# Differential attention's last heads: parts of dense units and output products placed around each transposition and ahead of each value product

## The chip, the core and the metric

The kernel runs on one core of a Trainium2 chip. The metric is the device time of one execution in microseconds. The kernel before takes 2173.66 us (median of three runs, 2173.38 to 2174.19). The core's engines have queues of their own and meet only at semaphores: TensorE (PE in the profile) multiplies and transposes into the eight PSUM banks, VectorE (DVE), ScalarE (ACT) and GpSimd (POOL) do the rest, and SyncE's queue (SP) starts the weight transfers.

## The reference, cut to what matters

The reference is a chain of a sparse-attention and latent-attention block, a recurrent (HGRN2) layer, two squared-ReLU MLPs and one layer of differential attention, for 512 positions of width 1024 in float32. The change is in the differential attention, which has 8 heads; the last two lines are in full what follows it before the last MLP.

```python
q = (h @ w_q).reshape(B, S, DIFF_HEADS, 2, DIFF_HEAD_DIM)
logits = einsum('bqhmd,bshmd->bhmqs', q, k) * scale + bias
logits = where(allowed, logits, NEG_INF)
p = softmax(logits, axis=-1)
attn = p[:, :, 0] - lam * p[:, :, 1]
o = einsum('bhqs,bshe->bqhe', attn, v)
o = rms_norm(o, subln_w) * (1.0 - lam_init)
mix = o.reshape(B, S, D_MODEL) @ w_out
h = h + rms_norm(mix, b_norm_post[bi])
```

## The kernel before, in words

Every engine's program is written out by hand, in the order in which its function calls stand; there is no planner. A float32 product of weights and activations is split: each weight unit (128x1024) is copied by ScalarE into a high part (`split` on ScalarE, line 935) and subtracted by VectorE into a low part (`split` on VectorE, line 1546), and TensorE multiplies three times (high by high, high by low, low by high). The split units lie in a ring of three buffers, `WHL`. The raw weights come by DMA into two slots of two units each, `raw`; a slot is free again when the low part of its second unit is made.

Differential attention goes head by head. For head h TensorE does, in this order:

- `map_scores(h, i)`, i = 0, 1, 2 (line 3004): the two maps' scores in pieces, read from PSUM by `biased_maps` on VectorE (line 2145), then `map_exp` on ScalarE (line 1397) and `joined` on VectorE (lines 2153 to 2161), which makes one map out of two.
- `turn_map(h, i)`, i = 0, 1, 2 (line 3017): ten 128x128 transpositions of the joined map, in groups of 4, 4 and 2. All three groups write the same bank, `TURN` (bank 1), so each waits until the one before has been copied out: the first two groups by ScalarE (`map_evac`, line 935, 128x512), the third by VectorE (`turned_map`, line 2170, 128x256).
- `map_values(h)` (line 3034): ten products of the turned map with the values, after all three copies.
- `map_out_turn(h)` (line 3042): four transpositions of the head's normed output. It needs the sums of squares (`map_squares`, ScalarE, line 1439), the root (`map_stats`, GpSimd, lines 721 to 725) and the scaling (`gated_map`, VectorE, line 2178). ScalarE then copies it out (`map_out_evac`), makes its high part (`map_x_high`), and VectorE its low part (`map_x_low`, line 2199). That is the left operand of the output product.

Between these small steps TensorE does dense work. For heads 0 to 5 this is `kv_dense(d)`, d = 0 to 39: the projections to keys, queries (`kq`, lines 2286 to 2288) and values (`dv`, lines 2984 to 2986), each call 12 products 128x512. The table `D_AT` says which calls belong to which head; `dense_at(h, i)` gives the i-th of up to six. Heads 0, 1, 2 have six, heads 3 and 4 five (d = 26 to 30 and 31 to 35), head 5 four (36 to 39): three go with the score pieces, the rest after the transpositions. So a head with five has nothing between its third transposition and its value product, and head 5 has nothing after its second transposition either. When a call with odd d is done, ScalarE (`kv_out`) copies a key or query out and splits a unit, and VectorE (`kv_low`) makes a low part.

For heads 6 and 7 the dense work is the output product `out_product(k, tts)` (lines 2882 to 2884), 12 products for all four row tiles, k = 0 to 15. For k below 8 it is the k-th head's output times the left half of `w_out`, and it waits for `map_x_low(k)`; k = 8 and up are the same heads with the right half. Two neighbouring k share a weight unit.

Of the kernel before, what the change touches and what calls it, by code (L numbers as in the profile page):

```python
# [37 lines left out]
KD = D // P  # L38
# [226 lines left out]
def program(nc, t, out):  # L265
    with ExitStack() as ctx:
# [146 lines left out]
        def dense_at(h, i):  # L413

            d = D_AT[h][0] + i if h < len(D_AT) else 0
            return d if h < len(D_AT) and d < D_AT[h][1] else None


        ss, rstd = small[:, 0:4], small[:, 4:8]
# [508 lines left out]
        def _(act):  # L928
# [5 lines left out]
            def copy(dst, src, **k):  # L934
                return a.activation(dst, src, ACT.Copy, **k)  # L935
# [464 lines left out]
            def map_evac(h, i):  # L1400

                if h >= 2 and i == 0:
                    act.wait_ge(pv_done, J_DIFF + h - 1)
                act.wait_ge(pt_psum, 3 * (J_DIFF + h) + i + 1)
                copy(map_turned(h)[:, 512 * i:512 * (i + 1)], TURN[:, :]).then_inc(pt_act, 1)
# [12 lines left out]
            def kv_out(d):  # L1418

                if d is not None and d % 2:  # L1420
                    name, u = DENSE_KV[d // 8], d // 2 % 4
                    if name[:2] == "kq":
                        key_query(name, u)
                    split(unit_at["dv0", 0] + d // 2 + HL)
# [31 lines left out]
            for h in range(HH - 2):  # L1456
                for i in range(3):
                    map_exp(h + 1, i)
                    if i == 2 and h:
                        map_out_evac(h - 1)  # L1460
                    kv_out(dense_at(h, i))
                map_evac(h, 0)
                kv_out(dense_at(h, 3))
                map_evac(h, 1)
                kv_out(dense_at(h, 4))
                kv_out(dense_at(h, 5))
                if h == HH - 3:
                    for k in range(4):
                        map_x_high(k)
                map_squares(h)  # L1470
# [27 lines left out]
        def _(vec):  # L1498
# [219 lines left out]
            for i, quarter in enumerate((0.25, 0.0)):  # L1718
                k = cs[:, 3 + i, :, :]
# [36 lines left out]
            for i in range(8):  # L1756
                s, tt = divmod(i, TT)
# [186 lines left out]
            for i in range(16):  # L1944
                half, rest = divmod(i, 8)
# [220 lines left out]
            def turned_map(h):  # L2166
                if h >= 2:
                    vec.wait_ge(pv_done, J_DIFF + h - 1)
                vec.wait_ge(pt_psum, 3 * (J_DIFF + h) + 3)
                v.tensor_copy(map_turned(h)[:, 1024:1280], TURN[:, 0:256]).then_inc(pt_vec, 1)  # L2170
# [21 lines left out]
            def kv_low(d):  # L2192

                if d is not None and d % 2:
                    split(w0 + d // 2 + 2)
# [17 lines left out]
            for h in range(HH - 2):  # L2213
                bias_ready(h + 1)
                for i in range(3):
                    biased_maps(h + 1, i)
                    if i == 0 and h == 4:
                        values_evac(1, (2, 3))
                    if i == 1 and h:
                        gated_map(h - 1)  # L2220
                    kv_low(dense_at(h, i))
                for i in (3, 4, 5):
                    kv_low(dense_at(h, i))
                turned_map(h)
                joined(h + 1)
                if h == 3:
                    values_evac(1, (0, 1))
# [30 lines left out]
        def _(pe):  # L2258
# [610 lines left out]
            def out_product(k, tts=range(TT), name="h_out"):  # L2869

                half, j, u = k // KD, k % 2, k // 2
                wh, wl = (y.rearrange("p (k c) -> p k c", k=2)[:, j, :] for y in unit(name, u))
                k %= KD
                if half == 0:
                    pe.wait_ge(x_lo, x0[name] + k + 1)
                for tt in tts:
                    if half == k == 0:
                        _, reader, at = GT["hg1" if name == "h_out" else "kq3"]
                        pe.wait_ge(ps_free[reader], at + tt + 1)
                    xh, xl = (y[:, k, tt * P:(tt + 1) * P] for y in (HXh, HXl))  # L2880
                    b = ybank(tt, half)
                    m.matmul(b[:, :], xh, wh, start=(k == 0), stop=False)  # L2882
                    m.matmul(b[:, :], xh, wl, start=False, stop=False)  # L2883
                    ins = m.matmul(b[:, :], xl, wh, start=False, stop=(k == KD - 1))  # L2884
                if tts[-1] == TT - 1 and j:
                    ins.then_inc(*((ring_used, 1) if u < KD - 1 else (y_full, 1)))
                elif half and k == KD - 1:
                    ins.then_inc(y_full, 1)
# [58 lines left out]

            norm_halves(5)

            def kv_dense(d):  # L2950

                c, half = divmod(d, 2)
                block, u = divmod(c, 4)
                name = DENSE_KV[block]

                def bank_free(i):

                    if half or u and name[:2] == "dv":
                        return
                    if block:  # L2960
                        _, reader, at = GT[DENSE_KV[block - 1]]
                        pe.wait_ge(ps_free[reader], at + i + 1)
                    elif i >= 2:
                        pe.wait_ge(ps_free["act"], GT["kq0"][2] + 2 * i - 3)

                if name[:2] == "kq":
                    w = [y.rearrange("p (k c) -> p k c", k=KD) for y in unit(name, u)]
                    bank_free(u)
                    for k in range(4 * half, 4 * half + 4):
                        ins = feature_product(DB[u], w, (HXh, HXl), k)  # L2970
                    if half:
                        ins.then_inc(ps_full, 1)
                    return
                wh, wl = (y.rearrange("p (k c) -> p k c", k=2) for y in unit(name, u))
                for tt in (2 * half, 2 * half + 1):
                    if u == 0:
                        if block:
                            _, reader, at = GT[DENSE_KV[block - 1]]
                            pe.wait_ge(ps_free[reader], at + tt + 1)
                        elif tt >= 2:  # L2980
                            pe.wait_ge(ps_free["act"], GT["kq0"][2] + 2 * tt - 3)
                    for k in range(2):
                        xh, xl = (y[:, 2 * u + k, tt * P:(tt + 1) * P] for y in (HXh, HXl))
                        m.matmul(DB[tt][:, :], xh, wh[:, k, :], start=(u + k == 0), stop=False)
                        m.matmul(DB[tt][:, :], xh, wl[:, k, :], start=False, stop=False)
                        ins = m.matmul(DB[tt][:, :], xl, wh[:, k, :], start=False, stop=(u == 3 and k == 1))
                    if u == 3:
                        ins.then_inc(ps_full, 1)
                    elif tt == TT - 1:
                        ins.then_inc(ring_used, 1)  # L2990
# [47 lines left out]
            def map_out_turn(h):  # L3038

                pe.wait_ge(on_ready, HH + h + 1)  # L3040
                for tt in range(TT):
                    ins = m.transpose(OUT[:, tt * P:(tt + 1) * P], on_d[:, h % 2, tt, :], ident[:, :])
                ins.then_inc(ot_psum, 1)

            def dense_step(h, i):

                d = dense_at(h, i)
                if d is not None:
                    kv_dense(d)
# [8 lines left out]
            for h in range(HH - 2):  # L3058
                for i in range(3):
                    map_scores(h + 1, i)  # L3060
                    if i == 2 and h:
                        map_out_turn(h - 1)
                    dense_step(h, i)
                for i in range(3):
                    turn_map(h, i)
                    dense_step(h, 3 + i)
                map_values(h)
            map_scores(7, 0)
            out_product(0, name="d_out")
# [2 lines left out]
            map_scores(7, 2)  # L3072
            map_out_turn(5)
            turn_map(6, 0)
            out_product(2, name="d_out")
            turn_map(6, 1)
            turn_map(6, 2)
            map_values(6)
            turn_map(7, 0)
            out_product(3, name="d_out")  # L3080
            turn_map(7, 1)
            map_out_turn(6)
            out_product(4, name="d_out")
            turn_map(7, 2)
            map_values(7)
            out_product(5, name="d_out")
            out_product(6, name="d_out")
            for k in (KD, KD + 1):
                out_product(k, (0, 1), "d_out")
            map_out_turn(7)  # L3090
            for k in (KD, KD + 1):
                out_product(k, (2,), "d_out")
            out_product(7, name="d_out")
# [37 lines left out]
```

## Time and profile before

| | |
|---|---|
| median of three runs | 2173.66 us |
| the profiled execution's own time | 2171.69 us |
| its span, first to last instruction | 2169.9 us |
| mean granted TensorE clock | 0.995 |
| TensorE busy, share of the span | 97% |
| VectorE, ScalarE, GpSimd busy | 49%, 38%, 13% |
| DMA, mean rate over the span | 88 GB/s |

A row of the timeline has the start in us from the span's start, the time in us that the instructions take together, engine, line, operation, output and input names, count, and in brackets the engine's idle time before it with what ended it. TensorE's rows overlap: a product of 512 columns is shown with 390 ns and the next starts earlier, so steps are measured from start to start. "Issue" as a releaser says that nothing the profile shows was seen to end the wait.

### The profile page before, as it was taken

What the parts mean: (1) busy time and instruction counts of PE and PEld (TensorE: products, weight loads), DVE (VectorE), ACT (ScalarE), POOL (GpSimd) and SP (SyncE); (2) the same over time, 40 slices, a digit from 0 to 9 for tenths busy, and PEclk for the clock granted to TensorE, in tenths of its full rate; (3) what the DMA queues carried; (4) which work ended last, traced back from release to release, by engine and by line L of the source; (5) the groups of instructions that cost most, each with busy time, mean ns of one, the idle gap of its engine ahead of it and who ended that gap; (6) DMA issues with size and microseconds to landing.
All of it is one profiled execution on the core that took longest, in us unless ns stands there. A gap on an engine that the chain in (4) does not pass through costs nothing.

```text
span 2169.9 us, 27018 instructions
## 1 busy us (share of the span) xinstructions
PE 2096.1 (97%) x10814; PEld 1722.8 (79%) x10814; DVE 1057.5 (49%) x1762; ACT 829.0 (38%) x1521; POOL 280.0 (13%) x337
## 2 busy tenths in 40 slices
PE   7999989999999999899999999999999989999998
PEld 6987557888887877788887888888877768888887
DVE  4442846565555343666665533433555546333334
ACT  3144745353333233423233422322445545223222
POOL 8300000010000000223232100000433101000000
PEclk9999999999999999999999999999999999999999
DMA  6435512323332222221212223222332212332222
GB/s 145 93 113 90 66 40 59 117 72 95 97 97 96 97 96 79 88 78 59 77 60 78 75 96 97 98 97 96 112 107 88 75 52 88 97 97 97 98 97 78
DMA packets 172346, 192.00 MB, mean 88 GB/s; under 512 B 22866, under 2 KB 141949, under 8 KB 172221
## 3 DMA queue, kind: packets, MB, share of 16 engines
q1 hardware_dynamic: 168301, 176.30, 26.1%
q0 software_dynamic: 3904, 13.97, 3.5%
q8 instruction: 86, 1.41, 0.3%
q14 instruction: 39, 0.32, 0.0%
q10 hardware_dynamic: 16, 0.00, 0.0%
HBM read 182.91 MB, written 7.34 MB: 88 GB/s over the span
## 4 chain that ended last, share of the span: by engine, by line
PE 91%; DVE 3%; ACT 2%; DMA 1%; issue 1%; POOL 1%; SPq 0%; POOLq 0%; ACTq 0%; DVEq 0%
PE bank L2416 25%; PE bank L2286 12%; PE bank L2288 12%; PE bank L2287 12%; PE bank L2826 2%; PE bank L2353 2%; PE bank L2354 2%; PE bank L2355 2%; PE bank L2861 1%; PE bank L2863 1%; PE bank L2862 1%; PE bank L2882 1%; PE bank L2884 1%; PE bank L2883 1%; PE bank L2555 1%
## 5 line engine op out<-in xcount | busy, mean ns | idle before, releaser
L1546 DVE TENSOR_TENSOR WHL<-raw,WHL 128x1024 fp32r<-128x1024 f32 x310 | 393.6, 1271 | 501.7 <-ACT WHL L935 501.4
L935 ACT ACTIVATE WHL<-raw 128x1024 fp32r<-128x1024 f32 x310 | 326.4, 1054 | 542.8 <-PE bank L2416 344.4
L2286 PE MATMUL bank<-HXh,WHL 128*128 128x512 f32 x1152 | 454.6, 395 | 2.7 <-DVE BIG L1762 1.6
L2288 PE MATMUL bank<-HXh,WHL 128*128 128x512 f32 x1152 | 449.7, 390 | 0.0
L2287 PE MATMUL bank<-HXl,WHL 128*128 128x512 f32 x960 | 373.6, 389 | 0.0
L2416 PE MATMUL bank<-WHL,HXh 128*128 128x512 f32 x1376 | 369.3, 390 | 0.7 <-ACT BIG L935 0.7
L2416 PEld LDWEIGHTS bank<-WHL,HXh 128*128 128x128 f32 x1376 | 257.7, 188 | 55.9 <-issue 1.9
L2286 PEld LDWEIGHTS bank<-HXh,WHL 128*128 128x128 f32 x1152 | 217.0, 188 | 51.0 <-issue 6.9
L2288 PEld LDWEIGHTS bank<-HXh,WHL 128*128 128x128 f32 x1152 | 216.8, 188 | 46.2
L2416 PE MATMUL bank<-WHL,HXl 128*128 128x512 f32 x688 | 211.9, 389 | 0.0
L2287 PEld LDWEIGHTS bank<-HXl,WHL 128*128 128x128 f32 x960 | 180.3, 188 | 36.6
L2416 PEld LDWEIGHTS bank<-WHL,HXl 128*128 128x128 f32 x688 | 129.1, 188 | 27.0
L2120 DVE TENSOR_TENSOR BIG<-PB 128x512 f32<-128x512 f32 x64 | 44.3, 692 | 192.1 <-ACT PB L1095 192.1
L737 POOL TENSOR_SCALAR small<-small 128x1 f32<-128x1 f32 x24 | 9.4, 393 | 954.0 <-ACT PB L1031 954.0
L1095 ACT ACTIVATE PB<-bank 128x512 f32<-128x512 f32 x64 | 38.2, 597 | 230.8 <-PE bank L2288 214.1
L1976 DVE SCALAR_TENSOR_TENSOR PB<-bank,cols,PB 128x511 f32<-128x511 f32 x88 | 65.9, 749 | 101.6 <-ACT PB L1310 100.0
L704 POOL TENSOR_TENSOR raw<-raw,cols 128x1024 f32<-128x1024 f32 x24 | 46.9, 1969 | 385.5 <-DMA raw<-in_b_w_q_dram 376.6
L1310 ACT ACTIVATE PB<-bank,cols 128x512 f32<-128x512 f32 x44 | 34.3, 781 | 142.0 <-PE bank L2288 136.1
L2416 PE MATMUL bank<-WHL,HX2h 128*128 128x512 f32 x352 | 83.2, 390 | 1.9 <-DVE HX2h L1555 1.7
L2416 PEld LDWEIGHTS bank<-WHL,HX2h 128*128 128x128 f32 x352 | 65.9, 188 | 16.4 <-issue 2.1
L2287 PE MATMUL bank<-HX2l,WHL 128*128 128x512 f32 x192 | 75.7, 394 | 0.0
L882 POOL TENSOR_TENSOR PB<-BIG,PB 128x512 f32<-128x512 f32 x24 | 40.1, 1671 | 174.7 <-PE bank L2826 121.7
(318 smaller groups left out, 3245.1 us busy)
## 6 DMA issues: line engine op xcount, KB each, us to landing
raw<-in_mlp_w_up_dram SPq DMA_DIRECT2D x64, 512.0 KB, 4.6
raw<-in_mlp_w_down_dram SPq DMA_DIRECT2D x64, 512.0 KB, 4.4
raw<-in_w_up_dram SPq DMA_DIRECT2D x44, 512.0 KB, 5.1
raw<-in_a_w_in_dram SPq DMA_DIRECT2D x32, 512.0 KB, 4.6
raw<-in_w_in_dram SPq DMA_DIRECT2D x24, 512.0 KB, 4.8
raw<-in_w_down_dram SPq DMA_DIRECT2D x22, 512.0 KB, 4.1
raw<-in_w_kv_dram SPq DMA_DIRECT2D x16, 512.0 KB, 4.2
rel_dram<-GB POOLq DMA_DIRECT2D x1, 5120.0 KB, 53.8
```

Source lines behind the costliest of these rows:

```text
L704: g.tensor_tensor(w, w, cols[:, c:c + nk].unsqueeze(2).to_broadcast([P, nk, D // nk]), ALU.mult).then_inc(w_scaled, 1)
L935: return a.activation(dst, src, ACT.Copy, **k)
L1546: v.tensor_tensor(dst(1), src, dst(0).bitcast(F32), ALU.subtract).then_inc(w_lo, 1)
L1976: ins = v.scalar_tensor_tensor(out=y[:, sh:T], in0=b[:, 0:T - sh], scalar=tapcol(tap, f), in1=y[:, sh:T], op0=ALU.mult, op1=ALU.add)
L2120: v.tensor_tensor(uT[:, f, :], r, r, ALU.mult).then_inc(u_ready, 1)
L2286: m.matmul(b[:, :], w[0][:, k, :], x[0][:, k, :], start=(k == 0), stop=False)
L2287: m.matmul(b[:, :], w[0][:, k, :], x[1][:, k, :], start=False, stop=False)
L2288: return m.matmul(b[:, :], w[1][:, k, :], x[0][:, k, :], start=False, stop=(k == KD - 1))
L2353: m.matmul(b[:, sl], wh[:, k, :], HXh[:, k, sl], start=(k == 0), stop=False)
L2354: m.matmul(b[:, sl], wh[:, k, :], HXl[:, k, sl], start=False, stop=False)
L2355: ins = m.matmul(b[:, sl], wl[:, k, :], HXh[:, k, sl], start=False, stop=(k == KD - 1))
L2416: ins = m.matmul(ybank(tt, h)[:, :], x, w[:, h * HALF:(h + 1) * HALF], start=(k == 0 and i == 0), stop=(k == nk - 1 and i == 2))
```

## The change

Nothing is computed differently and no instruction's shape changes. Two things move.

First, in the heads with fewer than six dense units the last unit is taken in two parts of six products each, one behind the transposition before its old place and one behind the transposition after. `parted(h)` names the position: 4 for heads 3 and 4 (d = 30 and d = 35), 3 for head 5 (d = 39), none for the others. ScalarE does head 5's `kv_out(39)` behind its second copy, and VectorE does `turned_map(h)` ahead of the `kv_low` of the parted position (that changes an instruction's place for heads 4 and 5; d = 30 has no `kv_low` work).

Second, in heads 6 and 7 the output products are halved by row tiles, (0, 1) and (2, 3), and spread; `out_product(4)` moves ahead of `map_out_turn(6)`, and a half of k = 9 moves behind `map_out_turn(7)`.

```diff
+        def parted(h):
+            return 5 - sum(dense_at(h, i) is None for i in (4, 5)) if dense_at(h, 5) is None else None
...
                 map_evac(h, 0)
-                kv_out(dense_at(h, 3))
+                if parted(h) != 3:
+                    kv_out(dense_at(h, 3))
                 map_evac(h, 1)
+                if parted(h) == 3:
+                    kv_out(dense_at(h, 3))
...
                 for i in (3, 4, 5):
+                    if i == (parted(h) or 6):
+                        turned_map(h)
                     kv_low(dense_at(h, i))
-                turned_map(h)
+                if parted(h) is None:
+                    turned_map(h)
                 joined(h + 1)
...
-            def kv_dense(d):
+            def kv_dense(d, part=None):
...
-                    bank_free(u)
-                    for k in range(4 * half, 4 * half + 4):
+                    if not part:
+                        bank_free(u)
+                    for k in range(4 * half + (2 if part == 1 else 0), 4 * half + (2 if part == 0 else 4)):
                         ins = feature_product(DB[u], w, (HXh, HXl), k)
-                    if half:
+                    if half and part != 0:
                         ins.then_inc(ps_full, 1)
...
-                for tt in (2 * half, 2 * half + 1):
+                for tt in (2 * half, 2 * half + 1) if part is None else (2 * half + part,):
...
                 for i in range(3):
                     turn_map(h, i)
-                    dense_step(h, 3 + i)
+                    if i + 2 == parted(h):
+                        kv_dense(dense_at(h, i + 2), 1)
+                    if i + 3 == parted(h):
+                        kv_dense(dense_at(h, i + 3), 0)
+                    else:
+                        dense_step(h, 3 + i)
                 map_values(h)
...
             turn_map(6, 0)
-            out_product(2, name="d_out")
+            out_product(2, (0, 1), "d_out")
             turn_map(6, 1)
+            out_product(2, (2, 3), "d_out")
             turn_map(6, 2)
+            out_product(3, (0, 1), "d_out")
             map_values(6)
             turn_map(7, 0)
-            out_product(3, name="d_out")
+            out_product(3, (2, 3), "d_out")
             turn_map(7, 1)
+            out_product(4, name="d_out")
             map_out_turn(6)
-            out_product(4, name="d_out")
             turn_map(7, 2)
+            out_product(5, (0, 1), "d_out")
             map_values(7)
-            out_product(5, name="d_out")
+            out_product(5, (2, 3), "d_out")
             out_product(6, name="d_out")
-            for k in (KD, KD + 1):
-                out_product(k, (0, 1), "d_out")
+            out_product(KD, (0, 1), "d_out")
             map_out_turn(7)
+            out_product(KD + 1, (0, 1), "d_out")
```

TensorE, head 5, before: the end of unit 39 (bank 2), the second and third group of transpositions (bank 1, together x6), the value product (bank 3), the scores of head 7 (banks 5 and 7) and the first output product (bank 4).

```order
L2286 MATMUL bank2<-HXh,WHL 128x512
L2287 MATMUL bank2<-HXl,WHL 128x512
L2288 MATMUL bank2<-HXh,WHL 128x512
L3017 MATMUL bank1<-ident,GM 128x128 x6
L3034 MATMUL bank3<-BIG,PB 128x128 x10
L3004 MATMUL bank5<-BIG 128x512
L3004 MATMUL bank7<-BIG 128x512
L2882 MATMUL bank4<-WHL,HXh 128x512
```

The same place in the changed kernel, from the second group of transpositions on (its line numbers are some ten higher).

```order
L3028 MATMUL bank1<-ident,GM 128x128 x4
L2296 MATMUL bank2<-HXh,WHL 128x512
L2297 MATMUL bank2<-HXl,WHL 128x512
L2298 MATMUL bank2<-HXh,WHL 128x512
L2296 MATMUL bank2<-HXh,WHL 128x512
L2297 MATMUL bank2<-HXl,WHL 128x512
L2298 MATMUL bank2<-HXh,WHL 128x512
L3028 MATMUL bank1<-ident,GM 128x128 x2
L3045 MATMUL bank3<-BIG,PB 128x128 x10
```

Six of unit 39's twelve products now stand between the second and the third group; between the third group and the value product there is still nothing.

VectorE, head 5, before: the low part of a weight unit, the copy of the third group (line 2170), the joining of head 6's maps (2153 to 2161) and the low parts of the first two heads' outputs (2199).

```order
L1546 TENSOR_TENSOR WHL<-raw,WHL 128x1024
L2170 COPY PB<-bank1 128x256
L2153 RECIPROCAL small<-small 128x8
L2156 SCALAR_TENSOR_TENSOR small<-small 128x4
L2161 SCALAR_TENSOR_TENSOR GM<-PB,small,GM 128x512
L2161 SCALAR_TENSOR_TENSOR GM<-PB,small,GM 128x384
L2161 SCALAR_TENSOR_TENSOR GM<-PB,small,GM 128x128
L2161 SCALAR_TENSOR_TENSOR GM<-PB,small,GM 128x256
L2199 TENSOR_TENSOR HXl<-BIG,HXh 128x512 x2
```

VectorE, head 5, in the changed kernel, from the copy on.

```order
L2177 COPY PB<-bank1 128x256
L1553 TENSOR_TENSOR WHL<-raw,WHL 128x1024
L2160 RECIPROCAL small<-small 128x8
L2163 SCALAR_TENSOR_TENSOR small<-small 128x4
L2168 SCALAR_TENSOR_TENSOR GM<-PB,small,GM 128x512
L2168 SCALAR_TENSOR_TENSOR GM<-PB,small,GM 128x384
L2168 SCALAR_TENSOR_TENSOR GM<-PB,small,GM 128x128
L2168 SCALAR_TENSOR_TENSOR GM<-PB,small,GM 128x256
L2206 TENSOR_TENSOR HXl<-BIG,HXh 128x512 x2
```

The low part of the weight unit has moved from ahead of the copy to behind it, and so ahead of the joining and of the two low parts of the output.

TensorE, head 7, in the changed kernel: the last products of `out_product(4)` (bank 2), the transposition of head 6's output (bank 3) head 7's third group and the first product of k = 5. Before, the bank-3 row stood directly behind the row of four on bank 1, and the twelve products behind it.

```order
L2892 MATMUL bank2<-WHL,HXh 128x512
L2893 MATMUL bank2<-WHL,HXh 128x512
L2894 MATMUL bank2<-WHL,HXl 128x512
L3053 MATMUL bank3<-ident,PB 128x128 x4
L3028 MATMUL bank1<-ident,GM 128x128 x2
L2892 MATMUL bank4<-WHL,HXh 128x512
```

## Rows read from the trace of the kernel before

**Rows 1.** The page: busy time by engine, and the chain that ended last by engine.

```profile
PE 2096.1 (97%) x10814; PEld 1722.8 (79%) x10814; DVE 1057.5 (49%) x1762; ACT 829.0 (38%) x1521; POOL 280.0 (13%) x337
...
PE 91%; DVE 3%; ACT 2%; DMA 1%; issue 1%; POOL 1%; SPq 0%; POOLq 0%; ACTq 0%; DVEq 0%
```

**Rows 2.** Timeline of PE, heads 2 and 3.

```profile
1672.96 0.38 PE L3017 MATMUL bank<-ident,GM 128*128 128x128 f32 x2
1675.93 2.39 PE L3034 MATMUL bank<-BIG,PB 128*128 128x128 f32 x20
1678.25 1.13 PE L3004 MATMUL bank<-BIG 64*128 64x512 f32 x4
...
1693.40 0.60 PE L3017 MATMUL bank<-ident,GM 128*128 128x128 f32 x4
...
1695.00 0.39 PE L2986 MATMUL bank<-WHL,HXl 128*128 128x512 f32 x1
...
1695.91 0.39 PE L2984 MATMUL bank<-WHL,HXh 128*128 128x512 f32 x1
...
1696.59 0.38 PE L3017 MATMUL bank<-ident,GM 128*128 128x128 f32 x2
1697.60 2.47 PE L3034 MATMUL bank<-BIG,PB 128*128 128x128 f32 x20 [0.63 <-issue]
```

**Rows 3.** Timeline of PE, head 5 to the first output product.

```profile
1734.13 0.60 PE L3017 MATMUL bank<-ident,GM 128*128 128x128 f32 x4
...
1737.34 0.60 PE L3017 MATMUL bank<-ident,GM 128*128 128x128 f32 x4
1739.62 0.44 PE L3017 MATMUL bank<-ident,GM 128*128 128x128 f32 x2 [1.68 <-ACT PB L935]
1740.69 3.72 PE L3034 MATMUL bank<-BIG,PB 128*128 128x128 f32 x20 [0.63 <-issue]
...
1745.75 0.50 PE L2882 MATMUL bank<-WHL,HXh 128*128 128x512 f32 x1
```

**Rows 4.** Timeline of PE, heads 6 and 7.

```profile
1753.85 0.60 PE L3017 MATMUL bank<-ident,GM 128*128 128x128 f32 x4
...
1759.41 2.47 PE L3034 MATMUL bank<-BIG,PB 128*128 128x128 f32 x20 [0.63 <-issue]
...
1767.76 0.66 PE L3042 MATMUL bank<-ident,PB 128*128 128x128 f32 x4 [2.19 <-DVE PB L2178]
...
1773.61 2.47 PE L3034 MATMUL bank<-BIG,PB 128*128 128x128 f32 x20 [0.63 <-issue]
...
1786.88 0.47 PE L2882 MATMUL bank<-WHL,HXh 128*128 128x512 f32 x1 [0.78 <-DVE HXl L2199]
```

**Rows 5.** Two windows: busy time by engine, then granted clock, DMA share, GB/s.

```profile
1740.00:1745.00 5.00, 4.37 (x23) 3.96 (x24) 4.04 (x11) 2.16 (x7) 0.00 (x0) 0.67 0.01 3
1770.00:1775.00 5.00, 4.37 (x21) 3.47 (x21) 1.02 (x2) 0.00 (x0) 0.00 (x0) 0.76 0.01 3
```

**Rows 6.** Timeline of ACT: copies of transposed maps of heads 5, 6 and 7.

```profile
1738.98 0.59 ACT L935 ACTIVATE PB<-bank 128x512 f32<-128x512 f32 x1
...
1755.40 0.58 ACT L935 ACTIVATE PB<-bank 128x512 f32<-128x512 f32 x1
...
1763.74 0.59 ACT L935 ACTIVATE PB<-bank 128x512 f32<-128x512 f32 x1
```

**Rows 7.** Timeline of DVE, head 5.

```profile
1731.91 1.23 DVE L1546 TENSOR_TENSOR WHL<-raw,WHL 128x1024 fp32r<-128x1024 f32 x1 [0.17 <-ACT WHL L935]
1740.17 0.42 DVE L2170 COPY PB<-bank 128x256 f32<-128x256 f32 x1 [7.03 <-PE bank L3017]
...
1742.85 1.29 DVE L2199 TENSOR_TENSOR HXl<-BIG,HXh 128x512 fp32r<-128x512 f32 x2
```

**Rows 8.** Line 721: xcount, duration ns min/median/max; and its longest, in the timeline of POOL.

```profile
L721 POOL TENSOR_SCALAR small<-small x8: 190/193/1243, 1633.1 to 1778.1; 128x4 f32<-128x4 f32 x8
...
1763.93 1.24 POOL L721 TENSOR_SCALAR small<-small 128x4 f32<-128x4 f32 x1 [15.90 <-ACT junk L1439]
```

## Prediction, made before the changed kernel had run

> **What bounds the kernel now.** I read the page first: TensorE is busy 97% of the span and 91% of the chain that ended last lies on it [rows 1]. So only time in which TensorE stands still, or runs at its lower clock, can be won, and all work of this change is there before and after in the same amount. Then the timeline of PE around the transpositions. In head 2 a whole unit stands between the third group and the value product, and nothing waits: from group to values 2.97 us [rows 2]. In head 3 nothing stands there, and values start 1.01 us after the group, 0.63 of it idle [rows 2]. In head 5 the third group waits 1.68 us and the values another 0.63 [rows 3]. In heads 6 and 7 there are idle times of 0.63, 2.19, 0.63 and 0.78 in the rows shown [rows 4]. Last the windows: the granted clock is 1.00 nearly everywhere, but 0.67 and 0.76 in two 5 us windows right behind the 1.68 and the 2.19 [rows 5]. There the value product takes 3.72 us, against 2.47 in head 3 and 2.39 in head 2 [rows 2, 3]. The two levels are 2.4 and 1.2 GHz, so part of each window ran at the lower one.
>
> **The yardstick.** Five dense products start from 1695.00 to 1695.91, four spacings of 0.227 us [rows 2]. Six products, half a unit, are 1.36. Taking half a unit out of a stretch of TensorE makes it 1.36 shorter, putting it in makes it so much longer, as long as no wait is met.
>
> **Heads 3 and 4.** In head 3 the second group starts at 1693.40, the third at 1696.59 (3.19, one unit between), the values at 1697.60: 4.20 in all [rows 2]. Afterwards half a unit is between groups: 3.19 - 1.36 = 1.83. Half a unit between the third group and the values: head 2's 2.97 - 1.36 = 1.61. Together 3.44, so 0.76 less; and a value product that follows work without a gap is 2.39 instead of 2.47, 0.08 less. Head 4 has the same shape. Both: 2 x 0.84 = 1.7. Do the copies fit? From the end of a group to the end of ScalarE's copy it is about 0.7 (a copy is 0.59 [rows 6] and starts within 0.1), and 1.83 less the group's own 0.60 leaves 1.23. VectorE's copy starts 0.55 after the third group and takes 0.42 [rows 3, 7], which is 0.97 of 1.61. In head 4 VectorE makes a low part behind the copy, and its joining for head 5 starts 1.2 later; it is wanted only at 1734, a dozen us on.
>
> **Head 5.** From the first group at 1734.13 to the first output product at 1745.75 are 11.62 [rows 3]. The 1.68 arises because ScalarE first copies the query of unit 39 and splits a unit, and comes to the group's copy at 1738.98, though the group began at 1737.34 [rows 3, 6]. Both causes go: ScalarE's two steps stand behind the copy, and half a unit covers it. The new sum: first to second group 3.21 - 1.36 = 1.85; second to third 1.83; third to values 1.01 as in head 3, since nothing covers it; values 2.40 and scores 1.06 to the next start (their 2.47 and 1.13 less the 0.07 by which rows overlap [rows 2]), at the full clock. That is 8.15. What is late next is VectorE: the first output product needs the first low part of the output. The copy of the third group starts at 1.85 + 1.83 + 0.55 = 4.23; from there to the low parts it was 2.68 (1740.17 to 1742.85), now plus the low part of a weight unit moved in between, 1.2; the first of the two takes 0.69 of their 1.29 [rows 7]. Ready at 4.23 + 2.68 + 1.2 + 0.69 = 8.8, so TensorE waits 0.65. Gain 11.62 - 8.8 = 2.8. The weights behind the moved low part are no risk: it frees the slot for those of k = 8 to 11, which are wanted only after the values of head 7, at 1773.61 before [rows 4].
>
> **From the first output product to k = 7.** Before: 1745.75 to 1786.88, 41.13 [rows 3, 4]. To head 6's first group it stays 8.10. From there to its values it was 5.56; now first to second group is 1.85 by products, but ScalarE's copy starts at 1755.40, 1.55 behind the group, and ends 0.58 later [rows 4, 6]: 2.18. Then 1.88 and 1.61: 5.67, with six more products done in it. Values 6 to values 7 took 14.20 [rows 4]. Now: ScalarE's squares of head 6 stand ahead of its copy of head 7's first group, which ends 1763.74 + 0.59 - 1759.41 = 4.92 behind the values' start [rows 4, 6]; second group at 4.97, where products alone would allow 4.2. Then a group and all of k = 4, 3.21; the transposed output of head 6 should be ready by then (it started 8.35 behind the values before [rows 4], 1.05 of it one slow GpSimd instruction [rows 8]; wanted at 4.97 + 3.21 = 8.18). Then 0.5, and 1.61 to the values: 10.3, where 2.19, 0.63 and the slow clock were. Values 7 to k = 7 took 13.27; now 36 products (8.17), values (2.25) and one output transposition (0.49): 10.9, since six products went ahead and the 0.78 is covered by the half of k = 9 behind the transposition. Sum 8.10 + 5.67 + 10.3 + 10.9 = 35.0. Gain 6.1.
>
> From k = 7 on the order is as before, and the MLP that follows hangs on TensorE alone.
>
> **Sum.** 1.7 + 2.8 + 6.1 = 10.6 us. The profiled execution took 2171.69; it should be 2161.1. The median of the runs lies 1.97 above that execution; by the same gain it comes to 2163.0, my forecast.
>
> **Unknown costs, from both sides.** The slow clock: it holds 1.25 of the values in head 5 (3.72 - 2.47), 0.35 of the scores behind, and about 1.6 in the stretch from 1767.76 to 1773.61 (5.85, where 3.21 + 1.01 = 4.22 were due). I take all 3.2 as won, because the idle times that stood ahead of both are cut to at most 0.8, and in heads 3 and 6 the 0.63 alone was followed by values at full speed [rows 2, 4]. If it all stays the gain is 7.4. If in addition some border elsewhere is spared, up to 1.6 more. The GpSimd instruction: line 721 has a median of 0.19 us and once took 1.24 [rows 8]. In the new order it meets VectorE's low parts again. Unblocked, head 6's output is ready 7.3 behind the values, blocked 8.35: a wait of 0 to 0.2. I take 0.
>
> The trace has the 1.24 us instruction running while VectorE makes low parts out of two SBUF inputs [rows 8]. The Trainium skill (SBUF — State Buffer, "Who interferes with whom") says that a VectorE instruction with two SBUF inputs and a GpSimd instruction that reads SBUF share a port and one blocks until the other ends. By that rule the wait is there again, at its length by chance; the sum moves by 0.2 at most.
>
> **Rivals.**
> (a) The clock drops in another place. The new order has more, shorter waits (0.6, 0.65, 0.3, 0.8), and everything behind is 10 us earlier, so idle times in the norms between stages fall elsewhere. For it: two windows did drop [rows 5]. Against: idle times under 0.8 had none. One or two drops at 1.6: 2164.6 to 2166.2. The Trainium skill (TensorE: Matmul & The Clock Gate, Part 1) says that the full clock is given only to a busy engine and judged at moments that do not follow the kernel; by it whether an idle time is punished is partly luck. The trace agrees in that the same 0.63 ahead of values was followed by 2.47 us three times and by 3.72 once [rows 2 to 4].
> (b) The shorter covers are too short: each of the eleven split places has only 1.2 to 1.6 us for a copy that passes a busy queue. At 0.4 us each, 4.4 are lost: 2167.4; at half the places 2165. Against: I found ScalarE free at all but two.
> (c) Given back later: the MLP waits for weights, or the norm for something fixed in time. Then 2170 to 2173.7. Against: the chain names DMA with 1% [rows 1].
> (d) Slower: with units cut to 1.36 us, TensorE stays at the lower level from the first output product to k = 7. 512 columns at 1.2 GHz are 0.43 instead of 0.227, so each of the 102 products there costs 0.2 more; 53 slow ones eat the gain, 75 make the kernel slower by over 0.2%, all would give 2183. For it only [rows 5]; each drop ended within its window.
> (e) That the change does nothing: the order of instructions shows the parts at their new places; no chance of its own.
>
> **How the numbers follow.** What a measurement of this kernel can tell from no change is about 0.2%, 4.3 us, so "faster" is below 2169.3. Forecast 0.60 (2161.4 to 2164.5); (a) 0.18; (b) 0.12; (c) 0.07; (d) 0.03. The range 2160.8 to 2167.2 takes in (a), most of (b) and a spared border. Faster: 0.60 + 0.18 + 0.12 and a little of (c), 0.92; same 0.05; slower 0.03.
>
> **What would show it.** Right: no idle time ahead of the values of heads 3, 4, 6 and 7; in head 5 the third group 1.8 behind the second, 0.63 ahead of the values and some 0.6 ahead of the first output product, with VectorE's low part as releaser; the clock at 1.00 in all windows from 1730 to 1780; k = 7 about 10.6 earlier than at 1786.88. Wrong: a window there below 0.9; waits for ScalarE's copy over 0.8; or a distance from k = 7 to the end that has grown.

## The result, and the profile after

The changed kernel's first six runs have a median of 2160.22 us (2157.02 to 2163.90), the kernel before, in six runs, 2173.67 (2173.38 to 2175.35): ratio 0.994, 95% interval 0.9929 to 0.9950. The forecast was 2163.0 in a range from 2160.8 to 2167.2. The direction was right; the median lies 0.6 below the range, and the gain, 13.4 us, was forecast as 10.6. The profiled execution took 2161.84, against the 2161.1 that the sum gave for it; 0.87 of it lies ahead of the change, as the marks below show.

The page of the changed kernel, its PE row and the chain that ended last; [rows 1] is the same of before. TensorE is busy 2.5 us less in a span 9.8 us shorter.

```profile
PE 2093.6 (97%) x10814; PEld 1721.1 (80%) x10814; DVE 1056.7 (49%) x1762; ACT 828.9 (38%) x1521; POOL 280.3 (13%) x337
...
PE 91%; DVE 4%; ACT 2%; issue 1%; DMA 1%; POOL 1%; SPq 0%; POOLq 0%; ACTq 0%; DVEq 0%
```

The timeline of PE, changed kernel. Head 3 first, to be read against [rows 2]: line 3028 is the groups of transpositions, 3045 the value product. From the second group to the third 1.86, to the values 1.66, and nothing idle; before, 3.19 and 1.01.

```profile
1691.06 0.60 PE L3028 MATMUL bank<-ident,GM 128*128 128x128 f32 x4
...
1694.27 0.60 PE L3028 MATMUL bank<-ident,GM 128*128 128x128 f32 x4
...
1696.13 0.44 PE L3028 MATMUL bank<-ident,GM 128*128 128x128 f32 x2
...
1697.79 2.39 PE L3045 MATMUL bank<-BIG,PB 128*128 128x128 f32 x20
```

Head 5, against [rows 3]. The 1.68 ahead of the third group is gone, the 0.63 ahead of the values is left, the values take 2.47 instead of 3.72, and there is a new idle time of 0.55 ahead of the first output product (line 2892).

```profile
1733.38 0.60 PE L3028 MATMUL bank<-ident,GM 128*128 128x128 f32 x4
...
1735.22 0.60 PE L3028 MATMUL bank<-ident,GM 128*128 128x128 f32 x4
...
1737.04 0.38 PE L3028 MATMUL bank<-ident,GM 128*128 128x128 f32 x2
...
1738.05 2.47 PE L3045 MATMUL bank<-BIG,PB 128*128 128x128 f32 x20 [0.63 <-issue]
...
1742.12 0.47 PE L2892 MATMUL bank<-WHL,HXh 128*128 128x512 f32 x1 [0.55 <-issue]
```

Heads 6 and 7, against [rows 4]: the first two groups of head 6 and its values, the second group of head 7, the turned output of head 6 (line 3053, without the 2.19) and the values of head 7 (without the 0.63). What is idle now is 0.19 and 0.68, both for ScalarE's copy.

```profile
1750.21 0.60 PE L3028 MATMUL bank<-ident,GM 128*128 128x128 f32 x4
...
1752.40 0.65 PE L3028 MATMUL bank<-ident,GM 128*128 128x128 f32 x4 [0.19 <-ACT PB L939]
...
1755.89 2.39 PE L3045 MATMUL bank<-BIG,PB 128*128 128x128 f32 x20
...
1760.79 0.66 PE L3028 MATMUL bank<-ident,GM 128*128 128x128 f32 x4 [0.68 <-ACT PB L939]
...
1764.06 0.60 PE L3053 MATMUL bank<-ident,PB 128*128 128x128 f32 x4
...
1766.10 2.39 PE L3045 MATMUL bank<-BIG,PB 128*128 128x128 f32 x20
```

The two windows of [rows 5], changed kernel: the granted clock (third number from the end) is full, 1.00, in both.

```profile
1740.00:1745.00 5.00, 4.45 (x21) 2.80 (x19) 4.08 (x12) 4.04 (x14) 1.41 (x3) 1.00 0.65 213
1770.00:1775.00 5.00, 5.00 (x26) 4.14 (x25) 2.26 (x5) 1.95 (x4) 1.40 (x3) 1.00 0.00 0
```

So the changed stretch does nearly what was forecast, wait by wait. To weigh it, three marks in the timeline of PE divide every profiled execution: the start of head 3's first group (1690.19 before, 1691.06 after), the first transposition behind the output product (the border) (1804.81 and 1794.94), and the end of the span. Between the first two lies the whole change: 114.62 before, 103.88 after, 10.7 less. From the border to the end it is 365.1 and 365.2. What is ahead of the first mark is the same program in both kernels, and came 0.87 later after.

```profile
1794.94 1.09 PE L2347 MATMUL bank<-ident,BIG 128*128 128x128 f32 x8 [1.33 <-DVE BIG L1514]
```

That leaves a question for the experiments: the stretch won 10.7, the six runs 13.4. Is the rest the order's doing, or chance?

### The profile page after: what moved, and what is told of

It reads as the page before. It is cut to its first block, busy times and chain, and to the rows that moved or that the text cites. A ratio compares the mean times of both kernels' runs of the same rounds, so it can differ in the third digit from the quotient of the medians.

```text
span 2160.1 us, 27021 instructions
## 1 busy us (share of the span) xinstructions
PE 2093.6 (97%) x10814; PEld 1721.1 (80%) x10814; DVE 1056.7 (49%) x1762; ACT 828.9 (38%) x1521; POOL 280.3 (13%) x337
## 4 chain that ended last, share of the span: by engine, by line
PE 91%; DVE 4%; ACT 2%; issue 1%; DMA 1%; POOL 1%; SPq 0%; POOLq 0%; ACTq 0%; DVEq 0%
PE bank L2426 25%; PE bank L2296 12%; PE bank L2298 12%; PE bank L2297 12%; PE bank L2836 2%; PE bank L2363 2%; PE bank L2364 2%; PE bank L2365 2%; PE bank L2871 1%; PE bank L2873 1%; PE bank L2872 1%; PE bank L2892 1%; PE bank L2894 1%; PE bank L2565 1%; PE bank L2893 1%; PE bank L2551 1%
```

## The experiments

**The kernel before again, and the changed kernel again.** No edit.

> The kernel before, unchanged, to see how its runs scatter and which mean clock each has. Theory A (the order gives 10.6 us, and the remaining 2.8 of the measured 13.4 are low-clock stretches that fall elsewhere in the program by chance): ratio 1.000, and the times of its runs fall as their mean granted clock rises, 0.001 of clock being some 2 us. Theory B (the order itself gives 13.4): its runs have the same clocks as those of the changed kernel and still lie 13.4 above them.

> The changed kernel again. Theory A: median 2159 to 2164, runs spread over 5 us or more with their clocks, and the runs whose clock is that of the kernel before (0.995) lie 10 to 11 below its profiled execution. Theory B: those of equal clock lie 13 below.

Measured: the kernel before 2173.77 (2170.04 to 2175.72, 11 runs), and a further 25 runs of it on the same chip 2173.20 (2168.02 to 2175.76); ratio 1.0005 (0.9996 to 1.0013). The changed kernel 2163.16 (2158.29 to 2164.66, 5 runs), ratio 0.9958 (0.9943 to 0.9972). Within each kernel the time falls as the mean granted clock rises: the runs before of 2168 to 2170 have 0.995 or 0.996, those of 2175 0.992 or 0.993; the changed kernel's of 2157 to 2159 have 0.996 or 0.997, those of 2162 to 2165 0.993 to 0.995. Over all runs of this study, fitted with one level for each kernel, a clock higher by 0.001 goes with 1.76 us less. Taken together, the 60 runs of before that were made beside the experiments, on three chips, have the median 2173.3 with a standard deviation of 2.5 (2173.5 with the first six), and the changed kernel's first 11 runs 2162.35 with 2.7: 10.9 to 11.1 apart. The second expectation asked for something more, that the changed kernel's runs with a clock of 0.995 lie 10 to 11 below the profiled execution of before. The two of them, 2161.84 and 2162.35, lie 9.9 and 9.3 below it, and by the fit over all runs it is 9.2. So that part missed. A likely reason, which no run tests, is that the two low-clock stretches that went are part of the gain, and a comparison at equal clock leaves them out. Theory A holds in its main point, theory B does not.

**Heads 3 to 5 alone, and heads 6 and 7 alone.** Each takes one half of the change; the other half stays as before.

The changed kernel's part for heads 6 and 7 undone (e3; the output products of k = 3, 8 and 9 go back in the same way):

```diff
             turn_map(6, 0)
-            out_product(2, (0, 1), "d_out")
+            out_product(2, name="d_out")
             turn_map(6, 1)
-            out_product(2, (2, 3), "d_out")
...
             turn_map(7, 1)
-            out_product(4, name="d_out")
             map_out_turn(6)
+            out_product(4, name="d_out")
             turn_map(7, 2)
-            out_product(5, (0, 1), "d_out")
             map_values(7)
-            out_product(5, (2, 3), "d_out")
+            out_product(5, name="d_out")
```

And its part for heads 3 to 5 undone (e4), on TensorE, ScalarE and VectorE:

```diff
                     turn_map(h, i)
-                    if i + 2 == parted(h):
-                        kv_dense(dense_at(h, i + 2), 1)
-                    if i + 3 == parted(h):
-                        kv_dense(dense_at(h, i + 3), 0)
-                    else:
-                        dense_step(h, 3 + i)
+                    dense_step(h, 3 + i)
...
                 map_evac(h, 0)
-                if parted(h) != 3:
-                    kv_out(dense_at(h, 3))
+                kv_out(dense_at(h, 3))
                 map_evac(h, 1)
-                if parted(h) == 3:
-                    kv_out(dense_at(h, 3))
...
                 for i in (3, 4, 5):
-                    if i == (parted(h) or 6):
-                        turned_map(h)
                     kv_low(dense_at(h, i))
-                if parted(h) is None:
-                    turned_map(h)
+                turned_map(h)
```

> Only the parts in heads 3 to 5 (units 30, 35, 39), heads 6 and 7 as before. By the sum of the prediction 1.7 + 2.8 = 4.5 us, so 2169.2 against 2173.7; rival (the parts give nothing on their own, the later waits take it back): 2173. In the trace k = 7 comes 4.5 earlier relative to head 3's first group: 92.2 instead of 96.7.

> Only the halved and moved output products of heads 6 and 7. By the sum of the prediction 6.1 us: 2167.6; from head 3's first group to k = 7 90.6 instead of 96.7. If the two parts are additive, e3 and e4 together make e2; if the clock decides, they differ from the sum by 1.6 or more.

Measured: 2166.71 (ratio 0.9972, 0.9962 to 0.9982) and 2167.19 (0.9975, 0.9965 to 0.9984). Between the marks: 108.58 and 108.29, so 6.1 and 6.4 less than 114.65, against forecasts of 4.5 and 6.1. The two sum to 12.4 where both together give 10.8, and e3's forecast was 1.6 too small. The surplus is the clock: in e3 the 2.19 us idle ahead of head 6's turned output is still there, but no low clock follows it. The 1.6 is the size that the prediction gave to the low-clock stretch there. The timeline of PE in e3:

```profile
1765.13 0.66 PE L3053 MATMUL bank<-ident,PB 128*128 128x128 f32 x4 [2.19 <-DVE PB L2185]
```

The window behind it, e3, with the clock at 1.00:

```profile
1770.00:1775.00 5.00, 5.00 (x32) 4.43 (x31) 0.00 (x0) 2.13 (x9) 1.00 (x2) 1.00 0.01 3
```

The values of head 7 then start 12.61 behind those of head 6, not 14.20 as in [rows 4]. So in these executions the low-clock stretch there, 1.6 us, is won by either half of the change, and counted twice in the sum of the two.

**ScalarE's order alone.** The kernel before, with one move.

```diff
                 map_evac(h, 0)
-                kv_out(dense_at(h, 3))
+                if h != 5:
+                    kv_out(dense_at(h, 3))
                 map_evac(h, 1)
+                if h == 5:
+                    kv_out(dense_at(h, 3))
```

> The kernel before with one move: on ScalarE, head 5's query copy and weight split (unit 39) stand behind the copy of the second transposed group. No product is moved. Theory (the 1.68 us ahead of head 5's third group were ScalarE's queue for 1.0 and the bare round trip for 0.7, and the slow values behind came from the long idle time): the third group waits 0.7 as in head 6, second to third group 1.3 instead of 2.28, and the values take 2.47: 1.0 + 1.6 = 2.6 us less between head 5's second group and the first output product. Rival (the half unit was needed, the queue did not matter): the idle time stays at 1.6 and nothing is won.

Measured: 2169.87 (ratio 0.9985, 0.9972 to 0.9998); between the marks 112.16, 2.5 less. From head 5's first group to the first output product it is 9.02 instead of 11.62, 2.6 less as forecast. Timeline of PE, head 5: the third group waits 0.69, the values take 2.47 at the full clock.

```profile
1739.34 0.60 PE L3020 MATMUL bank<-ident,GM 128*128 128x128 f32 x4
1740.62 0.44 PE L3020 MATMUL bank<-ident,GM 128*128 128x128 f32 x2 [0.69 <-ACT PB L935]
1741.70 2.47 PE L3037 MATMUL bank<-BIG,PB 128*128 128x128 f32 x20 [0.63 <-issue]
```

The theory holds and the rival falls. By itself this move of two instructions on ScalarE brings 2.6 of head 5's 2.9. On top of it the halves of unit 39 bring some 0.9 more, and VectorE's moved low part takes back 0.6 (e8, below). What the halves would bring without the move no run shows.

**The output product of k = 4 behind the turned output again.** The changed kernel, one part undone.

```diff
+            map_out_turn(6)
             out_product(4, name="d_out")
-            map_out_turn(6)
```

> The changed kernel with one part undone: the twelve products of k = 4 stand again behind the transposition of head 6's output. Theory: TensorE then waits for the scaled output, ready 7.3 (GpSimd unblocked) to 8.3 (blocked) behind the values of head 6, with the second group done at 5.5: idle 1.8 to 2.2, from values 6 to values 7 12.6 instead of 10.2; with a low-clock stretch behind it 14.2. Rival (the halves around the transpositions cover it): 10.5.

Measured: 2164.03 (2162.64 to 2170.74, ratio 0.9969, 0.9955 to 0.9983); between the marks 107.63, 3.8 more than the changed kernel. The median lies only 1.7 above the changed kernel's 2162.35, because the ten runs fall into two groups: six from 2162.64 to 2164.22 with a clock of 0.995 or 0.996, to which the profiled execution belongs, and four from 2168.29 to 2170.74 with 0.991 or 0.992. Their mean is 2166.0, 4.6 above the mean of the changed kernel's 11. No trace shows one of the four long ones. The timeline of PE in e6:

```profile
1754.48 2.39 PE L3045 MATMUL bank<-BIG,PB 128*128 128x128 f32 x20
...
1762.25 1.12 PE L3053 MATMUL bank<-ident,PB 128*128 128x128 f32 x4 [2.21 <-DVE PB L2185]
...
1766.96 0.38 PE L3028 MATMUL bank<-ident,GM 128*128 128x128 f32 x2
```

The window in which it falls, e6, with the clock at 0.70:

```profile
1760.00:1765.00 5.00, 2.79 (x10) 2.37 (x10) 2.26 (x5) 1.99 (x4) 0.96 (x2) 0.70 0.61 210
```

From the values of head 6 to those of head 7 it is 14.08: the idle time of 2.21 and the low clock (0.70) are both back. Of the parts that were undone or made one at a time, that one line is the largest between the marks.

**Three parts, and VectorE's low part later.** A kernel meant to be better than both: unit 39's half in three parts of four products, one behind each of head 5's groups (e7), and the low part of unit 39 behind the output's two low parts and no longer ahead of joined(6) (e7 and e8).

```diff
+                if part in ("a", "b", "c"):
+                    at = 4 * "abc".index(part)
+                    for n in range(at, at + 4):
...
                     turn_map(h, i)
+                    if parted(h) == 3:
+                        kv_dense(dense_at(h, 3), "abc"[i])
+                        continue
...
-                    kv_low(dense_at(h, i))
+                    if parted(h) != 3:
+                        kv_low(dense_at(h, i))
...
             map_x_low(0)
             map_x_low(1)
+            kv_low(dense_at(5, 3))
```

> The changed kernel, with head 5's unit 39 in three parts of four products, one behind each group of transpositions, and the low part of a weight unit, which had stood ahead of the joining, behind the low parts of the output. By the sum: first to second group 1.4, second to third 1.4, third to values 1.15, values and scores 2.32 + 1.06: 7.3 to the first output product instead of 8.74, so 1.4 less than the changed kernel from head 3's first group to the border (102.4 instead of 103.8). Rival (ScalarE's query copy, split and high part end too late now, since unit 39 ends later): a wait of 0.5 or more ahead of the first output product, and 0.9 less at most.

> The changed kernel with only the low part of the weight unit moved behind the low parts of the output in head 5. Theory (the moved low part makes the 0.55 us wait ahead of the first output product): that wait goes, 8.2 instead of 8.74. Rival (something else, as the query's copy out of the bank): it stays.

Measured, e8 (the last edit of the two alone): the idle time ahead of the first output product is gone, 8.13 from head 5's first group to it instead of 8.74, 103.23 between the marks. The theory holds. The timeline of DVE, e8, shows the low part (line 1553) behind the two low parts of the output (2206):

```profile
1738.63 1.29 DVE L2206 TENSOR_TENSOR HXl<-BIG,HXh 128x512 fp32r<-128x512 f32 x2
1739.83 1.22 DVE L1553 TENSOR_TENSOR WHL<-raw,WHL 128x1024 fp32r<-128x1024 f32 x1
```

e7: no idle time on TensorE from head 5's first group to the scores of head 7; 7.31 to the first output product, 102.33 between the marks, 1.5 less than the changed kernel (1.4 forecast), and 12.3 less than the kernel before. Timeline of PE, e7:

```profile
1734.00 0.60 PE L3042 MATMUL bank<-ident,GM 128*128 128x128 f32 x4
...
1735.37 0.64 PE L3042 MATMUL bank<-ident,GM 128*128 128x128 f32 x4
...
1736.77 0.38 PE L3042 MATMUL bank<-ident,GM 128*128 128x128 f32 x2
...
1737.92 2.39 PE L3059 MATMUL bank<-BIG,PB 128*128 128x128 f32 x20
...
1741.31 0.50 PE L2894 MATMUL bank<-WHL,HXh 128*128 128x512 f32 x1
```

Its runs, 2161.86 (2158.84 to 2164.07, six runs, ratio 0.9948, 0.9933 to 0.9963), cannot be told from the changed kernel's 2162.35. It beats the kernel before by more than its interval, and the changed kernel only between the marks of the trace.

**The clock again.** The e3 kernel in two more profiled executions and the changed kernel in one.

> The same kernel as in e3, one more look at the clock. In e3 TensorE stood idle for 2.19 us ahead of the transposition of head 6's output, as in the kernel before, and no low clock followed. Theory (whether an idle time is followed by the low clock is chance of when it falls): the stretch from the values of head 6 to those of head 7 takes 12.6 in one execution and 14.2 in another. Rival (the order makes it, since the work ahead of the idle time differs): 12.6 in each look.

> As e9, a further look: theory 12.6 or 14.2, rival 12.6 again. The start of head 3's first group, ahead of which all kernels of this study have the same instructions, moves by 1 us or more between looks under the theory that low-clock stretches further ahead come by chance.

> The changed kernel, one more look. From head 3's first group to the border 103.8 again, to within 0.1, and from the border to the end 365.1; only the time of head 3's first group differs from look to look (1689.5 to 1692.2 so far). Rival (the changed stretch itself scatters): 103.8 moves by 1 or more.

Measured: the values of head 7 start 12.64 and 12.60 behind those of head 6, as the rival has it. So in three profiled executions of this order the 2.2 us idle was not followed by the low clock. In the three where heads 6 and 7 stand as before but head 5's idle time or ScalarE's queue differs (before, e1, e5) it was, with 14.20, 14.18 and 14.21 from values to values, and in e6 too (14.08). That speaks for the order and against my theory of chance, but it doesn't decide: if four of the seven had been picked at random, they would have been just these in one case of 35, and e3 itself had raised the question, so that only two of the three are new.

The windows speak the other way. They show when the clock falls against the end of the idle time. The kernel before, where the idle time ends at 1767.76:

```profile
1767.00:1769.00 2.00, 1.25 (x8) 1.12 (x9) 1.83 (x4) 0.55 (x1) 0.00 (x0) 0.99 0.97 345
1769.00:1772.00 3.00, 3.00 (x9) 2.32 (x8) 0.00 (x0) 0.67 (x2) 0.00 (x0) 0.50 0.05 20
```

And e6, where it ends at 1762.25:

```profile
1760.00:1762.00 2.00, 0.04 (x1) 0.00 (x0) 0.93 (x4) 0.76 (x2) 0.96 (x2) 0.99 0.74 227
1762.00:1765.40 3.40, 3.15 (x10) 2.67 (x11) 1.33 (x2) 1.23 (x2) 0.00 (x0) 0.50 0.46 175
```

In windows of 0.1 us the clock falls 1.2 us behind the end of the idle time in the kernel before and in e1, 0.1 behind it in e5, and in e6 0.3 ahead of it, while TensorE still stands idle. So the moment of the fall does not follow the end of the idle time, and where an idle time lies against that moment may decide whether it counts. No run here moves one without the other. Why the same idle time is followed by the low clock in one order and not in the other stays open.

For the stretch ahead of head 3 the expectation of e10 holds. Between the marks the e3 kernel took 108.58, 108.62 and 108.54, the changed kernel 103.88, 103.77 and 103.78, the kernel before 114.62 and 114.69, and from the border to the end all 13 profiled executions 365.1 to 365.2. But the first mark stands anywhere from 1687.77 to 1693.47, with the same instructions ahead of it. Its start in the timeline of PE, in e9, the latest:

```profile
1693.47 0.60 PE L3028 MATMUL bank<-ident,GM 128*128 128x128 f32 x4
```

And in e10, the earliest:

```profile
1687.77 0.60 PE L3028 MATMUL bank<-ident,GM 128*128 128x128 f32 x4
```

Windows ahead of it, e9 (granted clock third from the end):

```profile
60.00:160.00 100.00, 96.67 (x837) 86.15 (x836) 35.66 (x99) 33.87 (x57) 15.21 (x30) 0.95 0.36 93
...
780.00:860.00 80.00, 74.72 (x332) 59.47 (x330) 29.23 (x32) 26.22 (x43) 4.82 (x10) 0.98 0.27 92
860.00:940.00 80.00, 73.48 (x429) 62.09 (x428) 50.08 (x64) 32.90 (x54) 18.40 (x24) 0.96 0.21 73
```

The same windows of e10:

```profile
60.00:160.00 100.00, 97.24 (x851) 86.98 (x850) 37.70 (x106) 33.99 (x57) 15.84 (x32) 0.98 0.36 93
...
780.00:860.00 80.00, 74.71 (x338) 59.48 (x337) 31.96 (x37) 26.44 (x45) 5.62 (x12) 1.00 0.28 92
860.00:940.00 80.00, 74.82 (x446) 63.40 (x445) 52.29 (x68) 33.46 (x54) 17.76 (x22) 0.98 0.24 80
```

The clock lost more in e9 by 100 x 0.03 + 80 x 0.02 + 80 x 0.02 = 6.2 us, to within some 1 us since the shares are rounded, and its mark is 5.7 later. It is most of the scatter, not all of it. Summed over windows of 5 us up to the mark, the missing share of the clock is 5.1 us in e10, 12.0 in e9, and in the other eleven between these. It goes with the mark (correlation 0.87), but e7 has the same 12.0 as e9 and its mark 1.8 earlier (1691.68). Why the clock falls once more or once less in the same program stretch no run shows.

## Why the prediction was wrong, and where it was right

- **Heads 3 and 4**: forecast 1.7, measured 1.6 (from head 3's first group to head 5's first group 43.94 before, 42.32 after). Head 4 came out as forecast. Head 3 took 1.86 and 1.66 where 1.83 and 1.61 were forecast. The prediction let ScalarE's copy start within 0.1 of the end of its group; that holds for the first group of head 3, but behind the second group ScalarE splits a weight unit first. The copy starts 0.62 behind the group's end and ends at 1696.07, and the third group starts at 1696.13: the cover just fits. The timeline of ACT, changed kernel:

```profile
1694.53 1.06 ACT L939 ACTIVATE WHL<-raw 128x1024 fp32r<-128x1024 f32 x1 [2.18 <-PE bank L2997]
1695.49 0.58 ACT L939 ACTIVATE PB<-bank 128x512 f32<-128x512 f32 x1
```

- **Head 5**: forecast 8.8 from 11.62, measured 8.74. The wait for VectorE's low part was forecast as 0.65 and is 0.55. The profile names nothing that ends it (issue), but in e8, with the low part moved away, it is gone.
- **To head 6's first group** 8.10 forecast, 8.09 measured; **to its values** 5.67 and 5.68, with a wait of 0.19 for 0.3; **to head 7's values** 10.3 and 10.21, with 0.68 for 0.8 at the place forecast; **to k = 7** 10.9 and 10.9. Sum 35.0 and 34.9.
- **The slow clock**: taken as wholly won, 3.2; both windows are at 1.00. In e3 the stretch at head 6 went although the idle time ahead of it stayed, so for that half the reason that was given, idle times cut to at most 0.8, is not the whole one.
- **GpSimd**: the instruction that was weighed took 0.72, until VectorE's low part ended (1761.06 against 1761.01), where its median is 0.19 [rows 8]. It cost nothing: the turned output of head 6 starts without an idle time. By the Trainium skill (SBUF — State Buffer, "Who interferes with whom") the two share a port; the trace agrees in that the GpSimd instruction ended with the other. The timeline of POOL, changed kernel:

```profile
1760.34 0.72 POOL L725 TENSOR_SCALAR small<-small 128x4 f32<-128x4 f32 x1 [16.01 <-ACT junk L1443]
```

And of DVE beside it:

```profile
1760.32 0.69 DVE L2206 TENSOR_TENSOR HXl<-BIG,HXh 128x512 fp32r<-128x512 f32 x1
```

- **The sum**: 10.6 forecast, 10.7 to 10.9 between the marks in three profiled executions of the changed kernel.
- **The step that failed** is the last: "The median of the runs lies 1.97 above that execution; by the same gain it comes to 2163.0", with a range whose lower end allowed for one spared low-clock stretch of 1.6. I read the 1.97 as a fixed distance between profile and runs. For the changed kernel it was -1.62 (2160.22 less 2161.84), and in the runs of e1 to e7 it lies between -1.4 and +1.6. It is a sample of a scatter, with a standard deviation of 2.5 us, mostly from low-clock stretches in the 1690 us ahead of the change, of which I had priced one. The three runs shown, within 0.8 us of each other, hid it; the profiled execution 1.7 below the lowest of them was the sign. The six runs after happened to hold three of the short kind (2157.02 to 2158.59, clock 0.996 or 0.997), and of the six before none lay below 2173.38. That is chance, not the order. With 60 and 11 runs the medians are 2173.3 and 2162.35. The mechanism and the size of the gain, 10.6, were right, and the forecast of 2163.0 lies 0.7 from the median of the 11; the range was too narrow for a median of six runs.
- **The rivals**: (a), new low-clock stretches behind the change, did not come: the stretch to the end kept its 365.1. (b), covers too short, at two of eleven places and 0.9 in all (0.19 and 0.68), where 0.3 and 0.8 were worked out. (c) and (d) not at all.

## What to carry to other kernels

Where one engine is the bound, its idle rows near the change, each with the queue of the engine that ends it, can give a change of order to a few tenths of a microsecond, as here; what the clock gives back they did not give, and one half of the change alone (e3) came out 1.6 off. Replay the order with start-to-start steps of the trace, and list for each wait what stands ahead of the releasing instruction. Look at that queue first: in head 5 two instructions moved on ScalarE brought 2.6 of the 2.9. Compare kernels between marks in the timeline around the change, and size the range of a median from the scatter of many runs, or from the distance between the profiled execution and the runs, not from three runs that agree.

## What the runs showed of the hardware

- The time of the same program on one chip scatters by 9 us (2167.70 to 2176.71 in 23 runs), and longer runs have a lower mean clock. In 13 profiled executions the first mark, with the same instructions ahead of it, stands at 1687.77 to 1693.47, and low-clock stretches ahead of it, missing 5.1 to 12.0 us of clock, make most of that.
- Idle times of up to 1.33 us behind the first mark were followed by no low-clock window in the profiled executions, except where one of 1.68 stood just ahead; 2.2 us were followed by one in three orders (four profiled executions) and by none in a fourth (three). The clock fell between 1.2 us behind the end of the idle time and 0.3 ahead of it.
